# Decayed HGRN keys transposed by DMA instead of TensorE, with the loads and weight copies of the first tiles rearranged

## Time and profile before

| | |
|---|---|
| Median of 3 runs | 3585.12 us (3565.34 to 4182.31) |
| Profiled execution | 3576.55 us, span of its slowest core 3575.5 us |
| Spans of the 8 cores | 3556.9 to 3575.5 us |
| TensorE busy | 3416.6 us, 96% of the span |
| VectorE, ScalarE, GpSimd busy | 38%, 35%, 22% |
| DMA engines, mean | 90% or more in the first 13 of 40 slices, around 50% after |

### The profile page before, as it was taken

How to read it: one execution, slowest core, us unless ns; L and a number is a source line. 1 busy time by engine, 2 the same in 40 slices (tenths; PEclk the granted TensorE clock), 3 DMA queues, 4 the chain that set the end, 5 groups by cost and what they waited for, 6 DMA issues and landing times.

```text
span 3575.5 us, 57595 instructions; the slowest of 8 cores (3556.9 to 3575.5 us)
## 1 busy us (share of the span) xinstructions
PE 3416.6 (96%) x18465; PEld 1623.2 (45%) x18768; DVE 1375.0 (38%) x3089; ACT 1268.5 (35%) x2303; POOL 802.4 (22%) x932
## 2 busy tenths in 40 slices
PE   3999879999999999999999999999999999999997
PEld 2444334444444444444444444444444444454443
DVE  1444124543345423354144442354324543345422
ACT  1345112643126331355214451254412643135421
POOL 1332313412233122220212211131112311122021
PEclk9999989999999999999999999999999999999999
DMA  9999989999897887645565445644446445454453
GB/s 233 204 173 203 202 170 237 229 214 230 217 261 212 223 229 220 218 137 195 194 199 182 161 174 178 228 163 165 177 177 230 159 170 178 170 188 132 154 183 136
DMA packets 171367, 688.80 MB, mean 193 GB/s; under 512 B 19776, under 2 KB 20032, under 8 KB 154688
## 3 DMA queue, kind: packets, MB, share of 16 engines
q1 hardware_dynamic: 137808, 563.96, 45.7%
q0 software_dynamic: 33264, 121.13, 21.6%
HBM read 711.75 MB, written 94.37 MB: 225 GB/s over the span
## 4 chain that ended last, share of the span: by engine, by line
PE 83%; DMA 10%; DVE 3%; ACT 2%; issue 2%; POOL 0%; DVEq 0%; SPq 0%; ACTq 0%; POOLq 0%
PE ps_pb L492 82%; DMA sb_Wb<-w_all 6%; DMA wsc<-sb_Wb 2%; DVE sb_arDE L903 2%; ACT L896 1%; DMA sb_Wb<-wsc 1%; ACT sb_arDE L896 0%; ACT sb_arDE L898 0%; PE ps_pb L669 0%; DMA sb_arDE<-x 0%; DVE sb_S L882 0%; DMA out<-sb_arDE 0%; POOL sb_Wb L113 0%; DVEq L82 0%; DVE sb_arDE L973 0%
## 5 line engine op out<-in xcount | busy, mean ns | idle before, releaser
L492 PE MATMUL ps_pb<-sb_arA,sb_Wb 128*128 128x512 bf16 x11217 | 2514.7, 380 | 39.7 <-DMA sb_Wb<-w_all 17.8
L492 PEld LDWEIGHTS ps_pb<-sb_arA,sb_Wb 128*128 128x128 bf16 x11520 | 1110.6, 98 | 1340.5 <-issue 47.8
L492 PE MATMUL ps_pb<-sb_Wb,sb_arB 128*128 128x512 bf16 x2048 | 448.4, 382 | 22.8 <-DMA sb_Wb<-w_all 19.2
L492 PEld LDWEIGHTS ps_pb<-sb_Wb,sb_arB 128*128 128x128 bf16 x2048 | 201.5, 98 | 268.7 <-issue 30.9
L941 DVE SCALAR_TENSOR_TENSOR sb_arDE<-sb_arDE,ps_pb 128x512 f32<-128x512 bf16 x128 | 88.0, 688 | 563.8 <-PE ps_pb L492 563.8
L492 PE MATMUL ps_pb<-sb_Wb,sb_arA 128*128 128x512 bf16 (+1 forms) x1536 | 282.6, 346 | 18.5 <-DMA sb_Wb<-w_all 18.5
L113 POOL DMA_DIRECT2D sb_Wb<-w_all x231 | 129.3, 562 | 674.4 <-PE ps_pb L492 554.6
L931 ACT ACTIVATE sb_arDE<-ps_pb 128x512 bf16<-128x512 f32 x128 | 75.5, 597 | 525.0 <-PE ps_pb L492 525.0
L639 POOL TENSOR_TENSOR sb_arDE<-sb_arDE,sb_Emb 128x512 bf16<-128x512 bf16 (+1 forms) x128 | 160.5, 1254 | 408.5 <-ACT sb_arDE L629 401.6
L944 POOL TENSOR_TENSOR sb_arB<-sb_arB,sb_arDE 128x512 bf16<-128x512 bf16 x128 | 148.2, 1158 | 401.8 <-DVE sb_arDE L941 401.8
L507 ACT ACTIVATE sb_tht<-ps_pb 128x512 f32<-128x512 f32 x192 | 114.4, 596 | 339.3 <-PE ps_pb L492 336.1
(11 more groups left out here) (97 smaller groups left out, 2424.5 us busy)
## 6 DMA issues: line engine op xcount, KB each, us to landing
sb_Wb<-wsc SPq DMA_DIRECT2D x697, 512.0 KB, 4.2
sb_Wb<-w_all POOLq DMA_DIRECT2D x231, 512.0 KB, 13.2
wsc<-sb_Wb SPq DMA_DIRECT2D x116, 512.0 KB, 9.8
sb_xb<-xt SPq DMA_DIRECT2D x32, 1024.0 KB, 9.1
out<-sb_arDE SPq DMA_DIRECT2D x31, 1024.0 KB, 6.5
sb_xb<-x SPq DMA_DIRECT2D x28, 1024.0 KB, 7.0
sb_arA<-x SPq DMA_DIRECT2D x8, 1024.0 KB, 6.4
sb_Vh<-x SPq DMA_DIRECT2D x8, 1024.0 KB, 7.5
```

What stands on the lines that cost most here:

```text
L492: return T.op("pe", lambda: PE.matmul(o, l, r_, start=start, stop=stop), r=r, w=w, signal=signal)
```

## The change

- `Kdtm` holds all four blocks, and a new `turn(h)` issues four DMA transposes of 128 x 128 bf16 (`sp_turn`) on SyncE's queue for each head: `turn(h-1)` behind `h2b(h)`, and `turn(7)` behind `h2b(7)`. `KdT` gets one buffer token per head. The 32 TensorE transposes and 8 ScalarE copies of a tile go.
- `wtile(u)` becomes a table. Counted from it: tile 0 converts 116 units and writes 22; tile 1 converts 94 and writes 43; tile 2 converts 51 and writes 26; tile 3 converts 25 and writes 25. In all 286 conversions instead of 231.
- Tile 0 does not load its x rows. The squares of `xt` are taken on ScalarE in 8 pieces, summed over features by 16 float32 matmuls with a matrix of ones, and the norm is made on ScalarE (Ln, Exp). Converting DMAs wait for the second quarter of `xt` (units 0 and 1) and the fourth (the rest). AV in all tiles runs k outermost over four banks.
- Three of the four bias loads and `npost` move into the attention of tile 0. `reload` of the residual rows is issued at j = 2 and 6 and in the first two WO groups instead of j = 0, 2, 4, 6. `x_sum` writes its unused squares into `Vh`. The last four quarters of the output get buffer tokens of their own.

```diff
+    def sp_turn(self, out, in_, dsem, r=(), w=()):
+        inst = self.nc.sync.dma_start_transpose(out=out, in_=in_)
...
         def wtile(u):
-            return min(u % 3, NTILES - 1)
+            if u < 24:
+                t_ = 0 if u >= 12 and u % 2 else 1
+            elif u < 52:
+                t_ = (2, 1, 2, 0, 2, 1, 2)[(u - 24) % 7]
+            elif u < 76:
+                t_ = u % 2
+            elif u < 100:
+                t_ = (3, 2, 3, 1, 3, 2, 3, 3)[(u - 76) % 8]
+            else:
+                t_ = (3, 2, 3, 1, 3, 2, 3, 3)[(u - 100) % 8]
+            return min(t_, NTILES - 1)
...
             if t == 0:
-                for b in range(4):
-                    x_rows(t, b, ysb[:, b, :], [Bys[b]], dx0[b])
-                for b in range(4):
-                    x_sum(b, ysb[:, b, :], [Bys[b]])
-                fill(2)
                 for q in range(4):
                     x_load(t, q)
-                for b in range(4):
-                    x_spread(b)
+                early_consts()
+                T._wait("pool", [Bxb[1]], [])
+                fill(2)
+                for q in range(4):
+                    for i in range(2):
+                        T.op("act", lambda: A.activation(out=ysb[:, q, cs], in_=xb[:, q, cs], func=AF.Square), ...)
+                    for i in range(4):
+                        mm(pb[6][:], rsb[:, 0, :], ysb[:, q, i * TT:(i + 1) * TT], ...)
+                T.op("act", ... func=AF.Ln ...); T.op("act", ... func=AF.Exp ...)
+                T._wait("pool", [Bxb[3]], [])
+                load_consts()
                 fill()
-                load_consts()
                 for q in range(4):
                     x_norm(q)
...
+            def turn(h):
+                for b in range(4):
+                    if b == 0:
+                        T._wait("sp", [BKdT[h]], [BKdtm[h]])
+                    T.sp_turn(Kdtm[:, h, b, :], KdT[:, h, bc], dKt[h], r=[BKdT[h]], w=[BKdtm[h]])
...
                 for hg in range(2):
-                    tb, ab = 7 - hg, 2 + hg
-                    for hh in range(4):
-                        T.op("pe", lambda: PE.transpose(ptbs[tb][:, hh, :], KdT[:, h, bc], ident[:]), ...)
+                    ab = 2 + hg
                     for hh in range(4):
                         mm(pb[ab][:, hh * 128:(hh + 1) * 128], KaT[:, h, bc], QaT[:, h, bc], True, True, ...)
-                    T.op("act", lambda: A.copy(Kdtm[:, 4 * hg:4 * hg + 4, :], ptbs[tb][:, 0:4, :]), ...)
...
-                if j % 2 == 0:
-                    reload(j // 2)
+                if j in (2, 6):
+                    reload(j // 4)
...
+                if i < 2:
+                    reload(2 + i)
...
+                bufs = [Bys[b]] if parts == 1 else [Buf(f"yq{i}") for i in range(parts)]
```

More of the change, by code:

```diff
@@ L294, in build_nc @@
         Byatm = [Buf("yatm0"), Buf("yatm1")]
-        Batt = BQT + BAGs + BPe + BPT + BPT2 + Byatm
+        BKdT = [Buf(f"KdT{h}") for h in range(8)]
+        Batt = BKdT + BQT + BAGs + BPe + BPT + BPT2 + Byatm
         arE = arDE[:, 9216:15360]
@@ L327, in build_nc @@
         dres = [T.dsem(f"dres{b}") for b in range(4)]
-        dx0 = [T.dsem(f"dx0{b}") for b in range(4)]
         KT = sb("KT", [128, 2, 640], BF16)
@@ L344, in build_nc @@
         BSb = [[Buf(f"Sb{h}_{i}") for i in range(2)] for h in range(8)]
-        Kdtm = sb("Kdtm", [128, 8, 128], BF16)
+        Kdtm = sb("Kdtm", [128, 8, 4, 128], BF16)
         BKdtm = [Buf(f"Kdtm{h}") for h in range(8)]
+        dKt = [T.dsem(f"dKt{h}") for h in range(8)]
         Am = sb("Am", [128, 8, 128], BF16)
@@ L391, in load_consts, with load_bias @@
             T.close_batch(dC2)
-            for i_ in range(4):
-                T.dma("sp", embv[i_], d_biasg[:, 1024 * i_:1024 * (i_ + 1)], dEb[i_], w=[Beb[i_]])
-            T.inherit(Bebv, Beb)
-            T.dma("sp", npost[:], d_npost, dC3, w=[Bnpost])
+            load_bias(0)
+        def load_bias(g):
+            T.dma("sp", embv[g], d_biasg[:, 1024 * g:1024 * (g + 1)], dEb[g], w=[Beb[g]])
+            T.inherit([Bebv[g]], [Beb[g]])
         def make_emb(g):
@@ L549, in do_tile @@
                 T.op("pool", lambda: G.memset(mhalf[:], -0.5), w=[Bmh])
[L550 to L556 removed]
+                T.op("pool", lambda: G.memset(rsb[:, 0, :], 1.0), w=[Brsb[0]])
+                T.dma("sp", npre[:], d_npre, dC, w=[Bnpre])
                 for q in range(4):
                     x_load(t, q)
[L559 to L560 removed]
+                early_consts()
+                T._wait("pool", [Bxb[1]], [])
+                fill(2)
+                Bx2 = [Buf(f"x2_{i}") for i in range(8)]
+                for q in range(4):
+                    for i in range(2):
+                        cs = slice(1024 * i, 1024 * (i + 1))
+                        T.op("act", lambda: A.activation(out=ysb[:, q, cs], in_=xb[:, q, cs], func=AF.Square),
+                             r=[Bxb[q]], w=[Bx2[2 * q + i]])
+                    for i in range(4):
+                        mm(pb[6][:], rsb[:, 0, :], ysb[:, q, i * TT:(i + 1) * TT], q == 0 and i == 0, q == 3 and i == 3,
+                           [Brsb[0], Bx2[2 * q + i // 2]], [Bpb[6]], signal=(i % 2 == 1))
+                T.inherit(Bys, Bx2)
+                T.op("act", lambda: A.activation(out=pb[6][:], in_=pb[6][:], func=AF.Ln, scale=1.0 / D, bias=epsb[:]),
+                     r=[Bc], w=[Bpb[6]])
+                T.op("act", lambda: A.activation(out=pb[6][:], in_=pb[6][:], func=AF.Exp, scale=-0.5), w=[Bpb[6]])
+                T._wait("pool", [Bxb[3]], [])
+                load_consts()
                 fill()
[L562 removed]
                 for q in range(4):
@@ L566, in do_tile @@
             wv, bw = wmov(["AV0", "AV1"])
-            for b in range(4):
-                bk = proj_bank()
-                for k in range(16):
+            banks = [proj_bank() for _ in range(4)]
+            for k in range(16):
+                for b, bk in enumerate(banks):
                     mm(pb[bk][:, 0:256].rearrange("p (u c) -> p u c", c=128), hT[:, k, b * 128:(b + 1) * 128],
                        wv[:, :, k, :], k == 0, k == 15, bw + [BhT[k]], [Bpb[bk]], signal=(k == 15))
+            for b, bk in enumerate(banks):
                 T.op("act", lambda: A.copy(Vaug[:, 1 + b, :, 0:64],
@@ L750, in h2b_guard @@
                 if not h2state["b"]:
-                    enter([BarD])
+                    enter([BarD] + BKdT)
                     h2state["b"] = True
                 h2b(h)
+                if h:
+                    turn(h - 1)
             def next_h():
@@ L773, in do_tile @@
                     gfill = [next_h, next_h, next_h, next_h]
+                if t == 0:
+                    if g < 3:
+                        load_bias(g + 1)
+                    else:
+                        T.dma("sp", npost[:], d_npost, T.dsem("dC3"), w=[Bnpost])
                 if nxt is not None:
@@ L795, in do_tile @@
             h2b_guard(7)
+            turn(7)
             pbanks[0] = (2, 3, 0, 1)
```

40 lines of the change are left out of this document (18 added, 22 removed).

## The result

**The changed kernel takes 3642.93 us as the median of 7 runs (3610.44 to 4185.57) against 3585.12 us before (7 runs, 3565.34 to 4183.44). The ratio is 1.0134, with an interval from 1.0093 to 1.0174: it is 1.3% slower.** That lies inside 2% and inside the range given, but on the other side of the forecast: 0.4% faster was predicted, 1.3% slower is measured, and the interval leaves out no change.

What follows compares the result with a forecast made beforehand. DMA was taken to pace tile 0 and just tile 1, TensorE tiles 2 to 7. Terms -41 - 10 + 20 + 2 + 7 + 9 + 17 - 4 + 3 - 8 = -5 gave 3571 us, range 3515 to 3655.

Steps and rivals of the forecast that it cites:

- Part 4: Key transposes on DMA: cost about their bytes, 3 us each in DMA-paced tiles 0 and 1; +3 us in all.
- I take the lower bound: DMA transposes: each 32 KB piece priced as a sixteenth of a 512 KB transfer, 0.1 us, 3 us a tile.
- rival 2: Section B of tiles 0 to 2: DMA transposes are slow, up to 49 us a tile, +123, 3691 us; chance 0.17.
- the 2% bound: Whole kernel: anything within 2%, 3513 to 3657 us, can't be told from no change.
- Part 1: New conversion table and x rows: tile 0 -41 us, tile 1 +20, +2 and +7, tile 2 +9, tile 3 +17.
- the x rows: Tile 0 loads none: 4.2 MB less DMA at 320 GB/s, within tile 0's -41 us.
- Part 2: The start: AV ends near 44 us instead of 46 and conversions are issued earlier; -10 us, bounds -14 and 0.
- rival 3: The start: float32 sums stay at the low clock, AV ends at 56 us, total 3582 us; chance 0.11.
- Part 3: Transposes off TensorE: it mostly waits longer for VectorE instead; only block 0 of each tile gains, -4 us.
- Part 5: The end: the last four output quarters no longer wait for each other's stores; -8 us.
- the signs named ahead: Predicted trace marks: tile windows, WO load waits, TensorE's wait near 0.8 us a block, transposes landing like small loads, output end.
- Rival 1: Late tiles absorb their conversions; tile 0 with the start gives 65 us, tile 1 +10, total 3512 us; chance 0.14.

Runs made afterwards that it cites:

- e5: The changed kernel with each DMA transpose replaced by a plain DMA of the same 128 x 128 piece, so keys are not transposed; ratio 1.0023.
- e3: The changed kernel with transposes back on TensorE and the old table of conversions; new start, moved loads, AV order and end kept; ratio 0.9962.
- e2: The changed kernel with the old table of conversions, DMA transposes kept; ratio 1.0038.
- e1: The changed kernel with the transposes back on TensorE and the new table of conversions kept; ratio 1.001.
- e9: The changed kernel with the old table and each transpose replaced by two tiny plain DMAs; no ratio, core median 3542.8 us.
- e6: The changed kernel with each DMA transpose replaced by three tiny plain DMAs; no ratio, core median 3573.7 us.
- e10: The changed kernel with DMA transposes and the old table, but units 24 to 51 converted in tiles 0 to 2 and written only in tile 2; ratio 1.0022.
- e14: The changed kernel with the old table, heads 0 to 3 transposed by DMA and 4 to 7 by TensorE; no ratio, runs 3581.81 to 3586.61 us.
- e4: The kernel before without its TensorE transposes of the keys and their ScalarE copies; ratio 1.0019.
- e7: The changed kernel with the KaT x QaT products in banks 6 and 7 instead of 2 and 3; ratio 1.0065.

## Why the prediction was wrong

**Part 4 failed.** "I take the lower bound" put 32 KB at a sixteenth of a 512 KB transfer, 0.1 us a piece and +3 in all. Measured are 27 us by the ratios with the old table, 44 with the new, 32 and 33 by the core medians, and 38 by the sections of either. The step's error is that it priced a transpose by its bytes, from rows of plain transfers. A plain DMA of the same piece does nearly cost its bytes in tiles 1 and 2 (e5), a transposed one does not. Even in a quiet tile a piece costs more than I took. Section B of tile 5 on core 2, e3, then e2, then e5, each 81.7 us long:

```profile
q1 hardware_dynamic: 3001, 10.92, 40.1%
...
sb_Wb<-wsc SPq DMA_DIRECT2D x21, 512.0 KB, 3.3
```

```profile
q1 hardware_dynamic: 8124, 11.98, 47.2%
...
sb_Wb<-wsc SPq DMA_DIRECT2D x21, 512.0 KB, 4.1
sb_Kdtm<-sb_arDE SPq DMA_TRANSPOSE x32, 2.4
```

```profile
q1 hardware_dynamic: 7631, 12.06, 46.5%
```

7.1% of 81.7 us are 5.8 us of all 16 engines for 32 transposed pieces, 0.18 us each, in some 160 packets a piece; e5's plain ones take 6.4%, 0.16 us each. So here the price is that of small packets, transposed or not. Beside converting loads the transposed pieces cost far more. Section B of tile 1 on core 2, e3 (81.7 us) and e2 (106.7 us):

```profile
q0 software_dynamic: 2160, 7.87, 60.5%
q1 hardware_dynamic: 2366, 8.59, 29.9%
...
sb_Wb<-w_all POOLq DMA_DIRECT2D x15, 512.0 KB, 11.6
sb_Wb<-wsc SPq DMA_DIRECT2D x8, 512.0 KB, 10.0
wsc<-sb_Wb SPq DMA_DIRECT2D x7, 512.0 KB, 10.1
```

```profile
q0 software_dynamic: 2170, 7.88, 55.7%
q1 hardware_dynamic: 7569, 9.94, 50.1%
...
sb_Wb<-w_all POOLq DMA_DIRECT2D x15, 512.0 KB, 17.4
wsc<-sb_Wb SPq DMA_DIRECT2D x8, 512.0 KB, 20.9
sb_Wb<-wsc SPq DMA_DIRECT2D x8, 512.0 KB, 18.4
sb_Kdtm<-sb_arDE SPq DMA_TRANSPOSE x32, 20.0
```

SyncE's queue holds the engines for 53.5 us instead of 24.4, for 1.35 MB more, and the 15 converting loads for 59.4 instead of 49.4 at the same bytes. By packet size, 9.9 of the 29 us are the pieces' own 256-byte packets and 16 are the 4 KB packets of the loads and writes beside them (40.6 for 24.5). So more of the price is paid by the neighbours than by the pieces. TensorE, which waits for nothing in that section of e3, waits in e2's (core 4; on core 2 it is 17.4 us in 4 waits):

```profile
PE ps_pb L500 <- DMA sb_Wb<-wsc: 10.2, 2, 7.3
```

This is rival 2 in place, direction and regime (B of the DMA-paced tiles, nothing in B later), at a smaller price: 21 and 16 us in tiles 0 and 1 with the old table, some 0.5 to 0.7 us a piece, where its bound was 49; with the new table 7.5, 19.1 and 10.8 in tiles 0 to 2. Its sentence "decides for slower from about 1 us per transpose on" used the 2% bound; half of that was enough for 1.3%. The rule of the Trainium skill that I set beside the term (Advanced Engine Details and Errata, X-Bar Transpose: as fast as regular DMAs) is borne out in the quiet section, 0.18 us a piece against 0.16, and not where it matters: beside converting loads, in the pair of e5 and the changed kernel, the pieces' own packets took 11.9 us for 5.3.

That the DMA transposes made the loss is shown, by undoing them with either table (e1, e3). What makes a transposed piece expensive beside converting loads is **not settled**. Excluded are the issue's own time on SyncE (e9, e6), bytes and packets in tiles 1 and 2 (e5; in tile 0 a plain piece cost nearly as much), and the scratch writes as a condition (e10: 14 us in tile 0 without any in B). The price is not proportional to the number (e14). Not tested is the queue held longer by issues that meet busy engines, 17 to 18 us a section in e2. Stalls inside the DMA engines would fit too; no run parts the two.

**Part 1, the table, held, with errors that cancelled.** With TensorE's transposes (e1 less e3): tile 0 -19.4 (the 22 writes for 39 were put at 8.9 MB, -28), tile 1 +27.3 (+29), tile 2 +0.8 (+9, bounds 0 and 16), tile 3 +13.7 (+17). In tile 2 the sum was wrong in its parts: D did lose 4.1 us (143.5 for 139.4), and A, which converts nothing now, gained 3.0, which the sum had at nothing. The sum is +22 by sections, +17 by ratios, and +27 was forecast. So by the forecast itself the table alone lost time, and with the -13 of the x rows Part 1 stood at +14. How tile 1's A loses is a chain that the sum did not name. Waits of core 4 in 519 to 653 us of the changed kernel, GpSimd's and then TensorE's:

```profile
POOL sb_Wb L113 <- DMA wsc<-sb_Wb: 45.3, 6, 13.1
```

```profile
PE ps_pb L510 <- POOL sb_arDE L666: 21.9, 2, 20.3
```

A slot comes free when its scratch write has landed; GpSimd waits there with the next converting load, its elementwise work for the attention (L666) stands behind that load in the same queue, and TensorE waits for L666. It is the table and not the transposes: the same section of e1 has 50.2 and 17.7 us of these two waits, that of e3 neither.

**Part 2, the start, held.** The float32 sums were out of the way at 26.4 us (rival 3, which had AV end at 56, fell), and AV ended at 42.2 us, with 44 forecast and 42 as the bound:

```profile
10.38 16.00 PE L510 MATMUL ps_pb<-sb_arDE,sb_rsb 128*128 128x512 f32 x32 [10.38 <-ACT sb_arDE L577]
...
18.88 3.17 POOL L113 DMA_DIRECT2D sb_Wb<-w_all  x6 [5.62 <-DMA sb_xb<-xt]
...
27.92 13.51 DVE L554 SCALAR_TENSOR_TENSOR sb_arA<-sb_xb,sb_npre,ps_pb 128x512 bf16<-128x512 f32 x16 [27.92 <-ACT ps_pb L585]
```

Against the earlier trace rows two of the first eight conversions leave 10.7 us earlier, at 11.97 for 22.64, and six 3.8, at 18.88. What it and the x rows gave was less than summed: K -3.5, tile 0 -17.2 and tile 1 +5.0 in e3 are -16, against -10 and -13. Tile 1's +5.0 lies in its D (145.4 us for 139.5), where the residual loads were moved, a step that the prediction put at nothing; no run parts it. One small cost was missed. AV with k outermost was put at nothing; its 64 matmuls take 7.15 us as before, but all four banks are done at the end, and K's product waits for ScalarE to copy them. Here are four tiles' waits of the changed kernel, in 1864 to 3350 us, where the kernel before has none; it is some 0.5 us a tile, 4 us in all:

```profile
PE ps_pb L510 <- ACT sb_Vaug L599: 2.3, 4, 0.8
```

**Part 3, transposes off TensorE, held by its mechanism.** -4 was forecast, 0.3 to 0.5 us a tile came (e4), because three blocks of four wait for the bank. The changed kernel shows the turn as the earlier trace rows; the second product comes 1.24 us late:

```profile
2097.12 0.38 PE L510 MATMUL ps_pb<-sb_QaT,sb_arDE 128*128 128x128 bf16 x4
2098.74 0.39 PE L510 MATMUL ps_pb<-sb_QaT,sb_arDE 128*128 128x128 bf16 x4 [1.24 <-DVE sb_arDE L940]
```

The forecast "grown to near 0.8 us" was a little low (0.96 on average). e7 turns it into a gain by using the freed banks.

**Part 5, the end, held.** The four quarters follow each other without a wait on core 4; from the first to the end of the span are 8.7 us, where 17.3 were before (3539.63 to 3556.9): -8.6 against -8. Compare:

```profile
3587.58 2.74 DVE L1012 SCALAR_TENSOR_TENSOR sb_arDE<-sb_arDE,sb_rs,sb_Gs 128x512 f32<-128x512 f32 x4 [0.99 <-POOL sb_rs L1002]
```

**The sum again**, by sections: -16 for start and x rows, +22 table, +38 transposes, +3 AV in tiles 2 to 7, -9 end: +38, against core 4's +39.4; the ratio's 1.34% are 48 us, by the slowest cores. With +3 for the transposes the same sum is +3, so Part 4 alone turns no change into slower. That the rest came out near the forecast's -5 is in part luck: start, x rows and tile 0's writes gave some 16 us less than summed, and the added conversions of tiles 1 to 3 cost some 13 us less. What Part 3 gained or lost in tiles 0 to 3 is inside the 38. Of the signs named ahead, tile 1 was to be longer by 25 us and was by 51, the transposes were to land like a small load and took 15 to 20 us beside converting loads, and tiles 2, 3 and 4 to 7 came near what was said (+12, +15, 427 to 430); tile 0 was to be shorter by 40 to 60 us and was by 29. Rival 1 fell with tile 3's +13.7; its 65 us for tile 0 with the start stand in no sum, for the terms give at most 41 and 14.
